# Row factors of seven RMS norms applied behind the matmuls instead of ahead of them

## What is computed

```python
def rms_norm(x, w):
    xf = x.astype(F32)
    y = xf * lax.rsqrt(jnp.mean(xf * xf, axis=-1, keepdims=True) + RMS_EPS)
    return (y * w.astype(F32)).astype(x.dtype)

def reference(...):
    h = x
    for i in range(DEPTH):                                   # DEPTH = 2
        hn = rms_norm(h, attn_norm_w[i])
        h = h + token_mixers(hn, w_in[i], ...)               # proj = hn @ w_in, ..., o @ w_out
        hn = rms_norm(h, ffn_norm_w[i])
        if i % 2 == 0:
            h = h + swiglu(hn, ffn_w1[j], ffn_w3[j], ffn_w2[j])
        else:
            h = h + moe_swiglu(hn, router_w[j], moe_w1[j], moe_w3[j], moe_w2[j])
        gate = jax.nn.sigmoid(rms_norm(h, ple_norm_w[i]) @ ple_gate[i])
        h = h + (p[i] @ ple_proj[i]) * gate
    return rms_norm(h, final_norm_w)
```

## Time and profile before

| | us |
|---|---|
| median of 3 runs | 1710.86 (1709.10 to 1712.62) |
| profiled execution | 1710.77 |
| its span in the trace | 1709.0 |
| PE busy in it | 1632.8 |
| DVE busy | 1296.2 |
| ACT busy | 1048.8 |
| POOL busy | 152.7 |

### The profile page before, as it was taken

One profiled execution on the slowest core, in us unless ns is written; L12 is line 12 of the kernel. 1 busy time (PEld: TensorE's weight loads), 2 busy tenths in 40 slices (PEclk: granted clock), 3 DMA queues, 4 the chain that ended last, 5 costly groups with the idle time before them and its releaser, 6 DMA issues.

```text
span 1709.0 us, 23469 instructions
## 1 busy us (share of the span) xinstructions
PE 1632.8 (96%) x8812; PEld 1391.7 (81%) x8812; DVE 1296.2 (76%) x1214; ACT 1048.8 (61%) x1005; POOL 152.7 (9%) x131
## 2 busy tenths in 40 slices
PE   6999989999899986999999999999999999999996
PEld 6989789998798975788888888888888888887875
DVE  5976555556697656688888888888889888888974
ACT  6656253334573724567777677767677777776754
POOL 0134100000012511000100101001001001002000
PEclk9999899999999987999999999999999999999998
DMA  8440164546444002999999999999999999999980
GB/s 312 149 148 1 58 217 158 218 154 223 170 150 171 2 28 96 338 367 355 395 362 357 394 361 365 382 366 376 373 355 388 368 357 388 366 358 404 376 331 25
DMA packets 65713, 459.91 MB, mean 269 GB/s; under 512 B 7408, under 2 KB 7792, under 8 KB 11632
## 3 DMA queue, kind: packets, MB, share of 16 engines
q1 hardware_dynamic: 61904, 445.88, 69.0%
q0 software_dynamic: 3744, 13.13, 2.0%
HBM read 450.58 MB, written 8.40 MB: 269 GB/s over the span
## 4 chain that ended last, share of the span: by engine, by line
PE 93%; ACT 2%; DVE 2%; DMA 1%; issue 1%; POOL 1%; DVEq 0%; POOLq 0%; ACTq 0%; SPq 0%
PE ps L1728 21%; PE ps L1732 20%; PE ps L1729 20%; PE ps L1721 6%; PE ps L1723 6%; PE ps L1722 6%; PE ps L1854 2%; PE ps L1863 2%; PE ps L2113 1%; PE ps L1923 1%; PE ps L1852 1%; DMA raw<-in_experts 1%; ACT whi L622 1%; ACT xh L859 1%; PE ps L1709 1%
## 5 line engine op out<-in xcount | busy, mean ns | idle before, releaser
L626 DVE TENSOR_TENSOR wlo<-raw,whi 128x2048 fp32r<-128x2048 f32 x421 | 945.1, 2288 | 106.4 <-ACT whi L622 106.1
L622 ACT CAST whi<-raw 128x2048 fp32r<-128x2048 f32 x421 | 784.7, 1917 | 73.9 <-DMA raw<-in_experts 73.6
L1728 PE MATMUL ps<-whi,xh 128*128 128x512 f32 (+2 forms) x1536 | 610.2, 398 | 14.3 <-ACT whi L622 9.1
L1729 PE MATMUL ps<-whi,xl 128*128 128x512 f32 (+2 forms) x1536 | 597.1, 389 | 0.0
L1732 PE MATMUL ps<-wlo,xh 128*128 128x512 f32 (+2 forms) x1536 | 415.2, 392 | 0.2 <-DVE wlo L626 0.2
L1728 PEld LDWEIGHTS ps<-whi,xh 128*128 128x128 f32 x1536 | 290.4, 189 | 83.2 <-issue 7.5
L1732 PEld LDWEIGHTS ps<-wlo,xh 128*128 128x128 f32 x1536 | 287.1, 189 | 66.6 <-DVE wlo L626 1.1
L1729 PEld LDWEIGHTS ps<-whi,xl 128*128 128x128 f32 x1536 | 290.6, 189 | 59.0
L1721 PE MATMUL ps<-xh,whi 128*128 128x256 f32 x656 | 186.4, 284 | 0.0
L1722 PE MATMUL ps<-xl,whi 128*128 128x256 f32 x656 | 185.0, 282 | 0.0
L1723 PE MATMUL ps<-xh,wlo 128*128 128x256 f32 x656 | 184.9, 282 | 0.0
(11 more groups left out here) (281 smaller groups left out, 1374.8 us busy)
## 6 DMA issues: line engine op xcount, KB each, us to landing
raw<-in_experts SPq DMA_DIRECT2D x336, 1024.0 KB, 5.1
raw<-in_stream SPq DMA_DIRECT2D x85, 1024.0 KB, 4.9
y_rows<-work POOLq DMA_DIRECT2D x7, 512.0 KB, 5.8
y_rows<-work POOLq DMA_DIRECT2D x1, 2560.0 KB, 10.6
cst<-in_consts SPq DMA_DIRECT2D x1, 1383.5 KB, 13.5
h<-in_x SPq DMA_DIRECT2D x1, 1024.0 KB, 4.9
x_rows<-hn POOLq DMA_DIRECT2D x1, 1024.0 KB, 4.4
out<-work SPq DMA_DIRECT2D x2, 512.0 KB, 2.7
```

The lines of the kernel that those rows point to most:

```text
L622: nc.scalar.copy(whi[:, n % RING, :], raw[:, n % RING, :]).then_inc(s_hi, 1)
L626: nc.vector.tensor_tensor(wlo[:, n % RING, :], raw[:, n % RING, :], whi[:, n % RING, :].bitcast(F32), ALU.subtract).then_inc(s_lo, 1)
L1728: pe.matmul(out, xu, wu, start=start, stop=False)
L1729: return pe.matmul(out, xd, wu, start=False, stop=False)
```

## The change

The factor is applied behind the matmuls, and each norm is cut in two halves of 512 columns (`EARLY`: PSUM tiles 0 and 1, `LATE`: 2 and 3).

- PE transposes `h` itself, without waiting for squares or factors, each half as soon as that half of the residual is added. The early half stands inside the stage before (`between=`), or between the halves of `PP`.
- ACT squares halves (`squares_of`), four instructions of 512 columns instead of two of 1024. POOL adds the half sums in one more instruction.
- Behind the matmuls: the token-major tiles are scaled by ACT as they leave PSUM. For the channel tiles PE makes a row of factors (`row_of_rstd`, two matmuls, three times in the program), ACT or DVE copies it to `rrow`, and POOL multiplies each of the 19 channel rows of a layer by it (`scaled_channels`). In the dense block DVE multiplies the left half of `H` by `rrow`, ACT takes silu in place, and the right half's factor is applied where `Y2` is added to the residual. The sigmoid of `PG` takes the factor as its scale. Router logits are scaled by DVE behind `LT`.
- All ten channel tiles are now taken by ACT, and `I` 7 stands ahead of the `N2` tiles on PE. In the dense block PE starts chunks 0 and 1 with the early half's channels.
- Splits stand at other places: behind the first half at the start, behind the first selection at the router, and ahead of the last transposed product in the last item (`most=2`), with those of the last loads moved ahead of the gated addition.

```diff
-            def norm(occ, items=None):
-                for c in range(4):
+            def turned_residual(occ, which, items=None):
+                residual_ready(pe, occ, NB - 1, which[0] // 2, items)
+                for c in which:
                     opened(("T", occ, c), items)
-                    if c == 0:
-                        pe.wait_ge(s_hn["a"], occ + 1)
-                        pe.wait_ge(s_hn["v"], occ + 1)
                     for q in range(4):
                         k, b = 2 * c + q // 2, q % 2
-                        ins = pe.transpose(bank(("T", occ, c), P * q, P), hn[:, b, P * k:P * k + P], ident)
+                        ins = pe.transpose(bank(("T", occ, c), P * q, P), h[:, b, P * k:P * k + P], ident)
                     ins.then_inc(s_fill, 1)
+
+            def row_of_rstd(key, occ):
+
+                opened(key)
+                pe.wait_ge(s_rstd, occ + 1)
+                for b in range(NB):
+                    ins = pe.matmul(bank(key, P * b, P), area("rstd", b, 1).broadcast_to([P, P]), ident, start=True, stop=True)
+                ins.then_inc(s_fill, 1)
...
+                def scaled_channels(first, end):
+
+                    for t in range(first, end):
+                        drained(pool, ("I", L, t), "a")
+                        own = [c for c in (2 * t, 2 * t + 1) if c < CQ + CA]
+                        for c in own:
+                            ins = nc.gpsimd.tensor_tensor(channel(c), channel(c), rrow, ALU.mult)
+                        ins.then_inc(s_scaled, 1)
+
+                scaled_channels(0, 5)
...
             def convolved(L, t):
 
-                drained(dve, ("I", L, t), "a")
+                dve.wait_ge(s_scaled, 10 * L + t + 1)
...
             for f in range(NF):
-                drained(dve, ("H", f), "a")
+                filled(dve, ("H", f))
+                nc.vector.tensor_tensor(ffs[f % 2], bank(("H", f), 0, T), rrow, ALU.mult).then_inc(s_ffa, 1)
+                dve.wait_ge(s_ffs, f + 1)
...
+            for f in range(2):
                 opened(("H", f))
                 ready(pe, ("w13", f))
...
+                dense_up(f, 0, early)
+                if f == 0:
+                    turned_residual(1, LATE)
...
             filled(act, ("LG",))
             nc.scalar.copy(logits, bank(("LG",), 0, T)[0:NE]).then_inc(s_free["a"], 1)
+            act.wait_ge(s_rstd, 5)
+            for b in range(NB):
+                nc.scalar.activation(hn[:, b, :], h[:, b, :], ACT.Copy, scale=area("rstd", b, 1)).then_inc(s_hn, 1)
             act.wait_ge(s_lsub, 1)
             nc.scalar.activation(exl, exl, ACT.Exp).then_inc(s_lex, 1)
+            split.behind(("WO", 1, 1, 1))
             split.behind(("LG",))
...
                 else:
                     scatter_matrix(it)
+                    split.behind(("B", ph, NJ - 1), it, most=2)
                 turned(ph, NJ - 1, it)
```

More of the change, by code:

```diff
@@ L877, in mixers @@
             def mixers(L):
-                norm(3 * L)
+                if L == 0:
+                    turned_residual(0, EARLY)
+                    split.behind(("T", 0, 3), most=1)
+                    turned_residual(0, LATE)
+                    split.behind(("T", 0, 3), most=1)
+                    squares_of(0, 0)
+                    squares_of(0, 1)
+                else:
+                    squares_of(3, 1)
+                    turned_residual(3, LATE)
                 split.behind(("T", 3 * L, 3))
@@ L913, in mixers @@
                     nc.scalar.activation(d, d, ACT.Exp).then_inc(s_dexp, 1)
-                split.behind(("I", L, 5))
+                channels(5)
                 silu(2)
@@ L925, in mixers @@
                                          bias=cc("eps")).then_inc(s_free["a"], 1)
-                split.behind(("I", L, 7))
+                channels(8)
                 for b in range(NB):
@@ L1100, in _ @@
             rest_of_item("last", items)
-            norm(5, items)
             ple(1, items)
-            norm(6)
+            squares_of(6, 1)
         @block.vector
@@ L1112, in step, with row_of_rstd, turned_residual @@
                 dve.wait_ge(st.sem, st.n)
-            def norm(occ, items=None):
-                dve.wait_ge(s_rstd, occ + 1)
-                nc.vector.tensor_scalar(hn[:, 1, :], h[:, 1, :], area("rstd", 1, 1), None, ALU.mult).then_inc(s_hn["v"], 1)
-                for c in range(4):
+            def row_of_rstd(key):
+                filled(dve, key)
+                nc.vector.tensor_copy(rrow, bank(key, 0, T)).then_inc(s_free["v"], 1)
+                drained(dve, key, "v")
+            def turned_residual(occ, which, items=None):
+                for c in which:
                     key = ("T", occ, c)
@@ L1396, in mixers @@
                 if L:
-                    residual_ready(dve, 3 * L, 1, None)
+                    residual_ready(dve, 3 * L, 1, 1, None)
                 nc.vector.memset(xc[:, :, 0:3], 0.0).then_inc(st.sem, st.up())
                 step()
-                norm(3 * L)
+                if L == 0:
+                    turned_residual(0, EARLY)
+                    split.behind(("T", 0, 3), most=1)
+                turned_residual(3 * L, LATE)
                 split.behind(("T", 3 * L, 3))
+                gates(L)
                 split.behind(("J", L, 1, 0))
-                gates(L)
                 for t in range(5):
@@ L1424, in mixers @@
                 qk_normalised(L, 2)
-                channels(9)
+                split.behind(("I", L, 9))
                 delta(L)
@@ L1432, in mixers @@
                         split.behind(("WO", L, 1, m))
+                    turned_residual(3 * L + 1, (EARLY, LATE)[m])
+                if L == 0:
+                    split.behind(("WO", L, 1, 1))
             def ple(L, items=None):
+                turned_residual(3 * L + 2, EARLY, items)
+                turned_residual(3 * L + 2, LATE, items)
                 split.behind(("PP", L, 1, 1), items)
@@ L1573, in _ @@
             first_selection()
+            split.behind(("WO", 1, 1, 1))
+            gathered("first", None)
+            split.behind(("LG",), most=1)
             nc.vector.tensor_scalar(over, cum[:, 16:24], P + 0.5, None, ALU.is_gt).then_inc(st.sem, st.up())
@@ L1610, in _ @@
             row_numbers()
+            split.behind(("LG",))
+            product("first", 0, None)
             def earlier_result(n):
@@ L1650, in rest_of_item @@
                     gathered(ph, it)
-                    split.behind(("B", ph, NJ - 1), it, most=2)
+                split.behind(("B", ph, NJ - 1), it, most=2)
                 turned(ph, NJ - 1, it)
@@ L1666, in rest_of_item @@
                             add_to_residual(("SC", b, m), b, m, it)
-            gathered("first", None)
-            split.behind(("LG",))
+                    split.behind(("YY", ph, 1), it)
             split.behind(("A", "first", 0))
-            product("first", 0, None)
             split.behind(("B", "first", 0))
@@ L1735, in x_part, with both_blocks @@
                 return xh[:, start:start + width], xl[:, start:start + width]
-            def both_blocks(keys, name, width, items=None, turned=None):
+            def both_blocks(keys, name, width, items=None, turned=None, between=None):
                 for half in range(2):
@@ L1746, in both_blocks @@
                             k = 4 * half + q
+                            if between is not None and (half, b, q) == between[0]:
+                                between[1]()
                             if b == 0:
@@ L1762, in projections, with token_major @@
             def projections(L):
[L1763 to L1766 removed]
+                def token_major(g, width, turned=None, between=None):
+                    both_blocks([("J", L, b, g) for b in range(NB)], ("J", L, g), width, None, turned, between)
+                late = ((0, 1, 2), lambda: turned_residual(3 * L, LATE)) if L else None
+                token_major(0, DG + 2 * HG, ("T", 3 * L), late)
+                row_of_rstd(("RB", L), 3 * L)
                 def channels(t):
@@ L2042, in _ @@
             mixers(1)
-            norm(4)
-            drained(pe, ("T", 4, 3), "v")
             opened(("LG",))
```

273 lines of the change are left out of this document (155 added, 118 removed).

## The result

The changed kernel takes 1686.82 us (median, runs from 1685.44 to 1687.14) where the kernel before takes 1710.48 beside it: a ratio of 0.9865, 95% interval 0.9847 to 0.9883. The forecast was 1679.5 with a range from 1673 to 1691. The time lies in the range, 7.3 us above the forecast: of a gain of 31.4 us, 23.7 came. The profiled execution shows 25.6 us (1709.0 to 1683.4).

What follows compares the result with a forecast made beforehand. PE was taken as nearly always busy, so time could come only from gaps between stages, chiefly at the norms. The terms summed to 31.4 us off the 1710.86 us median, giving 1679.5 us, range 1673 to 1691.

Steps and rivals of the forecast that it cites:

- The dense block and `PP`: Early transposes inside the stage before shorten PE's gaps: dense block 5.1 us (bounds 3.5 and 5.9), layer 0's gated addition 1.1.
- layer 1's mixer: `J` starts right behind `PG`, with the early half turned inside it; of the 8.74 us gap 1.94 remains: gain 6.8 us.
- the router: Between `WO` and the gathering matmuls, early transposes and later splits let DVE read logits sooner: gain 7.1 us (bounds 5 and 7.5).
- The last item and the gate: Waits for `whi` shrink or go at the last product and ahead of `PG`, with low-clock excess: 7.0 us (bounds 4 and 8).
- the start: PE's first transposes need only `h` and small inputs; first product at 11.8 instead of 16.70: 4.8 us taken.
- The rows of factors: PE makes three, two matmuls of 128 columns each at 0.12 us: a cost of 0.7 us in all.
- POOL's work: I take 0: In the convolutions, 19 POOL products can each delay DVE by 0 to 0.78 us; net cost taken as 0.
- 7 to 8 us against 6.1 + 2: Five pairs' delay to DVE in the convolutions against its 6.07 us idle and about 2 us of copies it loses.
- rival 1: DVE falls behind in the mixers: 7 us per layer, 14 in all, gives 1693; half of it 1686; chance 0.13.
- would show: Sign of DVE falling behind: PE waiting in the mixers for `N2`, `V` or `wlo`, and longer two-operand DVE instructions.
- Rivals 2, 3 and 4: Halves not hidden, 1693 (0.08); dense block a ping-pong, up to 1726 (0.04); another wait at each place, near 1708 (0.03).

Runs made afterwards that it cites:

- the last splits back: Changed kernel with ACT and DVE no longer splitting two weights ahead of turning the last product in the last item: 1688.16 us, ratio 0.9881.
- the table load first: Changed kernel with one tiny copy at the head of ACT's list, to load the activation table while the residual is on its way: 1687.11 us (one run).
- the other form of tap: Changed kernel with the convolutions' first tap as a scalar-tensor-tensor adding a row of zeros instead of a tensor-scalar: 1685.88 us, ratio 0.9854.

## Why the prediction was right or wrong

**Right: the chains at the norms.** The dense block and `PP` gave 6.4 (forecast 6.0), the start of layer 1's mixer 6.5 (6.5), the router 7.2 (7.1). The last item and the gate gave 8.6 against 7.2 with the tail. The step was to follow each gap to the next late thing, and it held where I had named that thing: `xl` in the dense block, with the wait of 0.86 us forecast as a short one, and the 2.4 us ahead of the expert product that stay. The inner split of the last term was nearly right too: I took 1.8 us for the item, and its stretch gave 2.4 (10.53 us from the last transposes to the scattering matmuls before, 8.13 after), of which its splits are 1.5; I took 5.2 for the gate, and it gave 5.7.

**Mis-sized: the start.** 4.8 was taken, 3.6 came. The sum had ACT's drain 1.12 us behind PE, in which the row of before showed no table load since that had long been done. What went missing is that the load is tied to the first ACT operation, and that the change put this operation behind a wait. The bound I named (the first load of weights landing late) wasn't it. The rows of factors were mis-sized a little as well: each takes PE 0.36 us (from 221.47 to 221.83, for one), 1.1 in all where I took 0.7.

**Wrong: "POOL's work: I take 0".** The single prices were right. I gave a DVE instruction up to 0.78 us of delay per POOL product, and the 19 of layer 1 cost 5.1 us, 0.27 each. What failed is the balance, "7 to 8 us against 6.1 + 2". The 6.07 us of the earlier trace rows are DVE's idle time ahead of `delta`, which is the end of its list; what PE needs first from that list is the last `wlo`, and that had 3.6 us to spare. The squares for `N2` had still less, 1.7 us in both layers (501.39 to 503.10 in layer 1): with GpSimd's work added to the kernel before, PE waited there 2.7 and 2.6 us. On the other side, the gates' later start stood in the rival's text at about 2 us, which is what it was (2.2), but not in this balance, which counted the 2 us that the copies save and nothing against them. And no price was on what a wait does to the clock: the 2.68 us cost 5.6 us more behind them.

So rival 1 came true in part, in the form that its "would show" named: PE waits for `wlo`, DVE's instructions are longer. It took 1.4 us in layer 0 and 9.3 in layer 1, 10.7 of the 14 that it had at full size. The total is short by less, since other stretches gave more than forecast: 1.4 us at the end, and 5.5 us between `C0` and `WO` in the two layers, which the forecast put at nothing and which I can't trace to the change (see the last section). **That is luck.** Without these 5.5 us this execution would have gained 20.1, and the median with 5.5 us more would be 1692, above the range. Rival 1 at half its size was put at 1686, which is nearly the time measured, but not in its way: three quarters of its price came off, and these 5.5 us came back. Rivals 2, 3 and 4 are out: no transposes wait for `h` but the first, and from the row of factors to `PG` of layer 0 PE took 186.9 us in the changed kernel and in every edit of it, without a wait in the loop. One reading of the prediction is wrong and bears on nothing: it speaks of three rows with nearly half of PE's waits, but the earlier trace rows are two, and their 29.8 us are 39% of the 76.2 that PE wasn't busy.

The Trainium skill's rule ("SBUF — State Buffer", Who interferes with whom) spoke against this part, and it would have been the better guide: DVE instructions with two SBUF inputs did take longer beside GpSimd's work (the pair of 1.82 us, and 2410 against 2284 ns for a split). The `TENSOR_SCALAR` has one such input and was slowed as much (695 against 349 ns). That page of the Trainium skill allows it for faster modes; no run here shows which mode it ran in.

## What to carry to other kernels

Measure slack (the time from when a result is ready to when it is wanted) at the thing that the bounding engine wants next, step by step down the other engine's list, and not as idle time at the list's end. When two engines share a helper, small delays of different causes add up until one wait shows; here any one of three, taken out, brought most of it back, so look for the cheapest (here one line moved). And price a wait on TensorE with the stretch behind it: here a list of short matmuls behind a wait of 2.7 us lost twice as much to the clock as to the wait.

## What the runs showed of the hardware

**A wait and the clock.** Waits for `wlo` ahead of `KK` of 0.74, 1.1, 1.4 and 1.8 us (the last two in layer 0 of the kernels with the last splits back and with the table load first) left `KK` to `C0` at 7.77 us. Behind those of 2.68 and 2.73 us (and two of 3.0 us in layer 1 of the same two kernels, with 13.44 and 13.46 us) the granted clock fell, which brought `KK` to `C0` from 7.77 to 13.4 us. One of 3.08 us, in layer 1 of the kernel with the other form of tap, did not lengthen that stretch: there the granted clock was 0.57 in the 3.95 us from the wait's end to `KK`, and 1.00 from `KK` on.

**The same waits, two clocks.** Around the start of `WO` PE waits 2.32 and 0.96 us in every trace for operands made from its own transposes. The same stretch of the kernel after in layer 0 and in layer 1:

```profile
185.29:191.29 6.00, 4.10 (x20) 1.00 0.00 0
611.50:617.50 6.00, 5.07 (x12) 0.52 0.01 3
```

From the first `WO` product to half 1 it takes 14.1 us or 16.5 us accordingly (the table's fifth column, 15.1 once), and which of the two changes from layer to layer of one execution. The way from `C0` to the first of these transposes varies likewise, from 74.3 to 76.5 us in the traces of the changed kernel and its edits, whose code there is the same. The kernel before took 76.0 and 76.5 us for this way and 16.4 and 16.5 for the other, the slow outcome in all four places; the changed one had it in one. That is the 5.5 us. What decides it stays open: PE's list between `C0` and half 1 is the same in both kernels, instruction for instruction, and so are the two waits. ACT has two splits fewer there in each layer of the changed kernel, so a part of the change in it isn't ruled out, though the edits show both outcomes with the same lists. For small differences this means that single traces are good for the time between two marks and poor for the total, and that totals are to be compared by the medians of several runs.
